# Attention steps of a fused two-block kernel: the values of a pair's first step are held back until those of its second

## What is computed

```python
# mixer A, one block of 128 queries over 512 keys (256 latents and 256 context)
s = jnp.einsum('bqhgd,bkhd->bhgqk', qi, k_all)
p = softmax_f32(s, v_all.dtype)
return jnp.einsum('bhgqk,bkhd->bqhgd', p, v_all)
# context queries, in the layers that need them
p = softmax_f32(jnp.einsum('bqhgd,bkhd->bhgqk', qcg, kc), vc.dtype)
yc = jnp.einsum('bhgqk,bkhd->bqhgd', p, vc)
# NSA: three branches of one head, each a masked softmax, gated and added
gate = jax.nn.sigmoid(g)
o = gate[..., 0:1] * o_cmp + gate[..., 1:2] * o_sel + gate[..., 2:3] * o_win
```

## Time and profile before

| what | value |
|---|---|
| median of three runs | 1896.64 us (1894.64 to 1898.02) |
| the profiled execution's own time | 1895.2 us |
| its span in the trace | 1893.4 us |
| PE busy | 1849.8 us, 98% of the span, 12748 matmuls |
| DVE busy | 1270.3 us, 67% |
| ACT busy | 1084.1 us, 57% |
| POOL busy | 95.9 us, 5% |
| turns L2422, 624 of them | 86.8 us busy, mean 280 ns |
| values L2452 of 128x128, 992 records | 69.6 us busy, mean 279 ns |
| spreads L2445, 88 of them | 21.7 us busy, mean 283 ns |
| ACT copies L1046 after turns | idle before them 83.3 us, 44 times, until L2422 |

### The profile page before, as it was taken

One profiled execution on the slowest core, in us unless ns is written; L12 is line 12 of the kernel. 1 busy time (PEld: TensorE's weight loads), 2 busy tenths in 40 slices (PEclk: granted clock), 3 DMA queues, 4 the chain that ended last, 5 costly groups with the idle time before them and its releaser, 6 DMA issues.

```text
span 1893.4 us, 33080 instructions
## 1 busy us (share of the span) xinstructions
PE 1849.8 (98%) x12748; PEld 1596.1 (84%) x12748; DVE 1270.3 (67%) x2139; ACT 1084.1 (57%) x1899; POOL 95.9 (5%) x83
## 2 busy tenths in 40 slices
PE   7999999999999999999999999999999999999998
PEld 5878878868788987888889988889888889998887
DVE  6663344477735569775677687767776677687765
ACT  5372264385726477774556567755774555567762
POOL 0000000004000005000000010000000000010001
PEclk9999999999999999999999999999999999999999
DMA  9232243232224213555532445545554542345443
GB/s 352 90 112 89 89 158 110 90 134 90 90 89 161 96 68 142 191 190 192 199 134 96 150 177 180 197 179 183 194 179 177 225 156 90 123 178 188 178 179 132
DMA packets 42565, 285.40 MB, mean 151 GB/s; under 512 B 4944, under 2 KB 6352, under 8 KB 9424
## 3 DMA queue, kind: packets, MB, share of 16 engines
q1 hardware_dynamic: 40832, 278.24, 40.4%
q0 software_dynamic: 1616, 5.52, 0.9%
HBM read 282.69 MB, written 1.05 MB: 150 GB/s over the span
## 4 chain that ended last, share of the span: by engine, by line
issue 49%; PE 41%; DVE 3%; POOL 3%; ACT 2%; DMA 1%; SPq 0%; DVEq 0%; POOLq 0%; ACTq 0%
PE bank L2211 7%; PE bank L2212 7%; PE bank L2213 7%; PE bank L2217 6%; PE bank L2218 3%; PE bank L2452 3%; PE bank L2422 2%; PE bank L2397 2%; POOL work L852 1%; PE bank L2313 1%; DVE panels_lo L1451 1%; DMA token_major<-weights 1%; POOL xT L895 1%; ACT work L1059 1%; ACT panels_hi L926 0%
## 5 line engine op out<-in xcount | busy, mean ns | idle before, releaser
L2217 PE MATMUL bank<-acts,panels_hi 128*128 128x512 f32 x2032 | 718.2, 399 | 3.5 <-DVE xT L1949 2.6
L1451 DVE TENSOR_TENSOR panels_lo<-raw_panels,panels_hi 128x1024 fp32r<-128x1024 f32 x468 | 577.8, 1252 | 186.6 <-ACT panels_hi L926 184.9
L926 ACT ACTIVATE panels_hi<-raw_panels 128x1024 fp32r<-128x1024 f32 x468 | 484.2, 1054 | 253.9 <-PE bank L2213 145.5
L2218 PE MATMUL bank<-acts,panels_lo 128*128 128x256 f32 x2032 | 569.4, 280 | 0.0
L2217 PEld LDWEIGHTS bank<-acts,panels_hi 128*128 128x128 f32 x2032 | 382.3, 188 | 98.1 <-DVE xT L1949 2.8
L2218 PEld LDWEIGHTS bank<-acts,panels_lo 128*128 128x128 f32 x2032 | 384.0, 189 | 0.2
L2211 PE MATMUL bank<-acts,panels_hi 128*128 128x256 f32 (+1 forms) x1112 | 349.5, 314 | 2.9 <-ACT gates L1403 1.2
L2212 PE MATMUL bank<-acts,panels_hi 128*128 128x256 f32 (+1 forms) x1112 | 344.3, 310 | 0.0
L2213 PE MATMUL bank<-acts,panels_lo 128*128 128x256 f32 (+1 forms) x1112 | 344.3, 310 | 0.0
L2211 PEld LDWEIGHTS bank<-acts,panels_hi 128*128 128x128 f32 x1112 | 211.8, 190 | 20.3 <-issue 3.9
L2213 PEld LDWEIGHTS bank<-acts,panels_lo 128*128 128x128 f32 x1112 | 211.9, 191 | 11.1
(11 more groups left out here) (282 smaller groups left out, 1961.0 us busy)
## 6 DMA issues: line engine op xcount, KB each, us to landing
raw_panels<-weights SPq DMA_DIRECT2D x252, 1024.0 KB, 4.8
token_major<-weights SPq DMA_DIRECT2D x4, 1024.0 KB, 8.7
near_bias<-rpb POOLq DMA_DIRECT2D x16, 256.0 KB, 3.4
xT<-xin SPq DMA_DIRECT2D x4, 512.0 KB, 5.9
gates<-weights SPq DMA_DIRECT2D x2, 1024.0 KB, 10.4
near_bias<-weights SPq DMA_DIRECT2D x4, 512.0 KB, 7.1
token_major<-weights SPq DMA_DIRECT2D x2, 512.0 KB, 12.8
out<-xT SPq DMA_DIRECT2D x4, 256.0 KB, 2.4
```

The costliest lines, as they stand in the source:

```text
L926: act.activation(slot_hi(n, a, b), raw_of(n, a, b), ACT.Copy).then_inc(hi_ready, 1)
L1451: dve.tensor_tensor(slot_lo(n, a, b), raw_of(n, a, b), slot_hi(n, a, b).bitcast(F32), ALU.subtract).then_inc(lo_ready, 1)
L2217: pe.matmul(bank.rearrange("p (c t) -> p c t", c=2), whi_, with_rest(xhi_), start=start, stop=False, skip_group_check=True)
L2218: return pe.matmul(bank[:, 0:T], wlo_, xhi_, start=False, stop=stop, skip_group_check=True)
```

## The change

In iteration i PE no longer issues spread and values of a pair's first step. It issues them one iteration later, with those of the second: first both spreads, then the values of the first step, then those of the second. Steps that are first and last at once stay where they were. No instruction is added or removed, and the code of ACT, DVE, POOL and SP is the same.

```diff
                 if blk == 2 and i == len(steps) + 2:
                     ahead(2)
-                if 0 <= j < len(steps):
+                if not 0 <= j < len(steps) or steps[j].first and not steps[j].last:
+                    ready = []
+                else:
+                    ready = [j] if steps[j].first else [j - 1, j]
+                for j in ready:
                     g, step = g0 + j, steps[j]
                     if late and j == 0:
                         pe.wait_ge(gate_last_out, late)
...
                         pe.wait_ge(normed, now(normed, 2 * g + 2))
                     for k, q0 in step.deferred:
                         pe.transpose(out_bank[:, T + q0:T + q0 + P], inverse_rows(blk, g, k), ident)
+                for j in ready:
+                    g, step = g0 + j, steps[j]
                     pe.wait_ge(probT_out, now(probT_out, g + 1))
                     if step.cmp:
                         pr = pairs[step.pair][0]
```

## The result

The changed kernel takes 1900.74 us (median of 20 runs, 1897.4 to 1905.83) against 1896.63 for the kernel before (20 runs, 1891.63 to 1902.44): a ratio of 1.0025, 95% interval 1.0017 to 1.0032, slower by 4.1 us. In a second group of runs it took 1902.2 against 1894.87, 1.0033 (1.0020 to 1.0046), 7.3 us. The forecast was +6.0. The profiled execution took 1900.34 us, its span is 1898.5 and its mean granted clock 0.996 (before: 1895.2, 1893.4, 0.998).

A forecast was written before the change was run, and what follows sets the result against it. PE, busy 98% of the span, was taken as the bound, with a 2.21 us floor from turns to turns through ACT's copy. 2.0 - 0.8 + 4.6 + 0.2 = +6.0 us gave 1902.6 us; 8-in-10 range 1898.5 to 1907.

The forecast's parts named there:

- (1): PE, every pair: fewer changes of tile shape, 0.09 us each; 2.9 us saved over 32 pairs at one change each.
- (2): PE's wait for the previous pair's output goes; 1.8 us idle in all until L1630, 0.38 of it at 419.14.
- (4): End of mixer C, layer 0: values hide in a wait for ACT and the output wait goes, -0.8 us.
- (3): Layer 0: ten bare iterations with scores behind cost +0.20 us a pair, +2.0 in all; copy's wait for values hidden.
- the bare iteration: Odd iteration left without spread and values: turns to turns takes 2.21 us, set by ACT's copy, for 1.92 of work.
- (5): Layer 1 mixers: first even turns stay put, values come after them; A +1.69, B +1.59, C +1.32, together +4.6 us.
- the pins: Layer 1 mixers: first even turns come no earlier if PE arrives earlier, as ACT rounds panels before its copy.
- (6): NSA: waits of 0 to 0.1 us against 0.09 saved, last pair about +0.4 a layer; +0.2 for both layers.
- Rival (c): NSA: ACT's later rounding delays the gates of all eight pairs, +4 to +6 us on top, 1908 us; chance 0.12.
- Rival (a): PE's scores and other work cover ACT's copy; only (1) and (2) are left, 1892 us; chance 0.06.
- Rival (b): Slack after mixers absorbs half the shift in layer 1 and A, B of layer 0: +2.9, 1899.5 us; chance 0.16.

The follow-up runs named there:

- e5: The change with values held back but not grouped (spread, values, spread, values): 1907.87 us, ratio 1.0064 to the kernel before.
- e2: The change with ACT's copy of the turned probabilities cut in two, one piece per head and bank: 1889.79 us, ratio 0.9975 to the kernel before.
- e4: The change with a third buffer for the copied probabilities in the first block: 1898.35 us, ratio 1.0025 to the kernel before.
- e1: The change, but with layer 1 of the first block left as before: 1895.46 us, ratio 1.0001 to the kernel before.
- e6: The change with a gate panel's rounding and split three iterations later in the first block: 1902.74 us, ratio 1.0042 to the kernel before.
- e9: The change with ACT's copy cut in two and a third probability buffer in the first block: 1887.61 us, ratio 0.9961 to the kernel before.
- e12: The change with cut copy and third buffer, values held back everywhere but in C of layer 1: 1889.31 us, ratio 0.9967 to the kernel before.
- e10: The kernel before with cut copy and third buffer, no values held back: 1891.03 us, ratio 0.9978 to the kernel before.
- e11: The change with cut copy and third buffer, values not held back in A of layer 0 and C of layer 1: 1889.76 us, ratio 0.9984.
- e8: The change run again without any edit: 1902.2 us, ratio 1.0033 to the kernel before.

## Why the prediction was right

The sign, the mechanism and the size held: +4.1 and +7.3 measured for +6.0, inside the range. By its steps:

- **(1) changes of shape, mis-sized.** I took 0.09 us for one change. Grouped, the stretch takes 2.20 and not the 2.26 I used, and ungrouped 2.51 (e5): two changes are worth 0.31. The Trainium skill, "TensorEngine Tiling (Array Packing)", Key Properties, says that a switch of mode drains TensorE and gives no size; here it is 0.15 between transposes and values. My 0.09 came from turns with scores behind them, another pair of shapes.
- **(2) waits for the output.** The one of 0.38 us at the end of C in layer 0 went. But the waits of spreads for L1630 fell only from 1.8 to 1.4, and I had written "nearly gone" as a sign: what is left stands in front of single steps (128.80, 132.41 and 292.16 in the changed trace). The sum used only the first, in (4).
- **(3) the bare iteration** is 2.21 to 2.22 us in 9 of the 10 places in layer 0 and at the second pair of all three mixers in layer 1, and cutting the copy brings 1.92 (e2). A pair in B of layer 0 costs 0.14 to 0.16 more (7.66 us for 7.50 to 7.52), forecast 0.20. In A of layer 0 three pairs cost as little, and the fourth, with its bare iteration of 3.16 us, 0.35. Its copy's wait for values is not hidden, because a rounding follows it on ACT, and costs 0.44 (e4); I had put this wait at nothing. So +0.73 for +0.8 in A is partly luck, B came at +0.57.
- **(4) end of C, layer 0**: the stage came at -0.54 for -0.4.
- **(5) layer 1**: the pins held to 0.01 us in A and C, counted from the start of the stage. From them, two pairs take 12.50 us in both (502.10 to 514.60 in A), forecast 12.60, and what stands behind came 0.24 shorter than I had it: four changes of shape at 0.15 and not 0.09. Together A +1.35 for +1.69, C +0.98 for +1.32. In B the pin did not hold: in e4 its first even turns come 4.37 us after the turns before, in the kernel before 4.63. That gives +0.96 (e4, no fall of the clock) for +1.59.
- **(6) NSA** came at -0.25 for +0.2. The wait at the last pair is there, as forecast: in the first of the two NSA stages it takes 0.30 us more than before (forecast about 0.4). But each of the other three pairs takes 0.14 to 0.16 less, where I had waits of 0 to 0.1 against a saving of 0.09. Rival (c), the NSA chain turned critical, did not appear.

Without the fall of the clock the stages sum to +3.8 (the change's row with e4's B of layer 1), 2.2 under the forecast. Most of it is (1): the mis-sized changes of shape make up 1.0 in layer 1 and about 0.06 a pair in layer 0, and very likely the NSA difference too, where nothing but shapes and waits changed. The uncovered wait in A of layer 0 went the other way. On top came a term that no step had, the clock in B of layer 1: that stage is 1.1 us longer than e4's in one profile and 3.1 in the other, of which 0.9 and 2.8 lie in the one stretch (from turns to turns 4.98 and 6.83 us, 4.04 in e4) in which the clock was low. The two errors have opposite signs, and part of the accuracy is their cancelling.

Rival (a), that the copy never bites, is what happens once the copy is cut; for this kernel spoke rightly against it. Rival (b) fell by e1 and by the distances between the stages.

## What to carry to other kernels

Work that looks movable on the bound engine may be what fills a chain through another engine: before moving it, compute the distance from each product to the next that reuses its banks without it. If that distance is set by one evacuation of several banks, cut the evacuation per bank first; here grouping products of one shape paid only then. Look also at what the other engine has in front of that evacuation: the places where this change cost more than its sum said had a rounding there. And read a small change off stages that repeat to 0.02 us, not off whole executions.

## What the runs showed of the hardware that I had not expected

**TensorE's clock can fall where its waits stand close together.** PE in mixer B of layer 1 of the changed kernel, and the time slices (stretch, its length, busy time and count of PE, PEld, DVE, ACT, POOL, then the granted clock, DMA share, GB/s):

```profile
604.06 1.09 PE L2422 MATMUL bank<-consts_sb,work 128*128 128x128 f32 x8 [0.23 <-ACT token_major L1046]
606.71 1.32 PE L2397 MATMUL bank<-kT_split,qT_split 64*128 64x512 f32 x6 [1.56 <-ACT work L1059]
608.57 1.97 PE L2422 MATMUL bank<-consts_sb,work 128*128 128x128 f32 x8 [0.54 <-ACT token_major L1046]
```

```profile
604.00:606.00 2.00, 1.09 (x8) 0.86 (x8) 1.58 (x5) 0.80 (x4) 0.00 (x0) 1.00 0.01 4
606.00:608.00 2.00, 1.29 (x6) 0.56 (x6) 1.79 (x9) 2.00 (x4) 0.54 (x1) 0.78 0.29 76
608.00:610.00 2.00, 1.46 (x9) 1.43 (x8) 2.00 (x5) 2.00 (x6) 0.54 (x1) 0.50 0.45 104
610.00:612.00 2.00, 2.00 (x27) 1.82 (x27) 1.90 (x5) 0.85 (x2) 0.54 (x1) 0.87 0.20 82
```

PE is busy 2.38 of the 4 us from 604, then the grant is 0.50, that is 1.2 instead of 2.4 GHz, and eight turns with what follows take 1.76 us (608.57 to 610.33) and not 0.94. The kernel before has a spread and values there:

```profile
604.53 0.33 PE L2445 MATMUL bank<-consts_sb,token_major 128*128 128x128 f32 x1 [1.12 <-DVE gates L1694]
604.79 1.09 PE L2452 MATMUL bank<-token_major 128*64 128x128 f32 x16
```

and its clock stays at 1.00 in this stage. In the change's second profile it fell again and for longer:

```profile
606.00:608.00 2.00, 0.97 (x6) 0.49 (x6) 1.89 (x8) 2.00 (x6) 0.54 (x1) 0.94 0.21 35
608.00:610.00 2.00, 1.29 (x6) 1.29 (x7) 1.86 (x3) 2.00 (x6) 0.54 (x1) 0.50 0.56 162
610.00:612.00 2.00, 2.00 (x16) 1.67 (x16) 1.90 (x7) 0.94 (x1) 0.54 (x1) 0.50 0.16 66
612.00:614.00 2.00, 2.00 (x22) 2.00 (x20) 0.39 (x1) 0.88 (x1) 0.00 (x0) 0.50 0.79 184
```

Of the five profiles with values held back in this stage and the copy in one piece, three have the fall there (the change twice, e6); none of the other nine has. That the missing values are the cause is the likely reading, not a shown one. It doesn't come each time: in e4 PE was busy 0.66 and 1.02 us in the two slices from 604 to 608 and the grant stayed at 1.00. A fall at the start of A of layer 1 (e5, e6, e9, e12) stands behind an idle time of PE of 1.8 us (493.61 to 495.40 in the kernel before) that the change has too. It came in four of the nine profiles that hold values back in that stage and in none of the five that don't; but it starts ahead of the first place where the holding back changes anything in the stage, so whether the two are connected is open.

**The same products run at one of two paces at full grant.** 100 us of the second block, the stretches from 760 and from 1140 us, in the kernel before:

```profile
760.00:860.00 100.00, 100.00 (x569) 86.68 (x568) 74.84 (x100) 67.80 (x98) 0.00 (x0) 1.00 0.53 189
1140.00:1240.00 100.00, 100.00 (x579) 87.42 (x578) 79.00 (x109) 73.42 (x109) 0.00 (x0) 1.00 0.52 189
```

and in the changed one:

```profile
760.00:860.00 100.00, 100.00 (x579) 88.15 (x578) 77.08 (x105) 70.95 (x104) 0.00 (x0) 1.00 0.55 197
1140.00:1240.00 100.00, 100.00 (x568) 86.69 (x567) 77.11 (x107) 72.38 (x107) 0.00 (x0) 1.00 0.52 188
```

569 or 579 matmuls, 1.8% apart, with a grant of 1.00 in all and no work of the change in either. All fourteen profiles show one of the two paces in each stretch (567 to 569 or 578 to 579), and the distances to the attention stages follow it:

| from | to | fast pace | slow pace |
|---|---|---|---|
| last values of C, layer 1 | first NSA scores | 278.9 to 279.2 us | 281.5 to 281.6 us |
| last values of the first NSA and MoBA stage | next NSA scores | 497.0 us | 500.2 us |
| last values of the second | end of the span | 242.3 to 242.4 us | 245.5 to 245.6 us |

A fall of the clock near 960 us (e10, e11) or near 1550 us (e5, e10, e12) adds 1.4 to 1.7 us to its row; the one that ten profiles show between 711 and 727 us, both kernels among them, adds nothing that can be seen. For the third I did not count matmuls; it takes one of two lengths, 3.2 us apart. The three together are 9 us between all fast and all slow, and that is where most of the 8 to 11 us between single executions of one kernel can come from. The kernel before and the change show it: their spans differ by 5.1 us, the stages by 4.9, and between them lie -2.6 and +3.2 from two stretches whose pace changed, and -0.4 ahead of the first stage. e9's profile (span 1884.4) is fast in all three, that of e10 (span 1897.0) slow in all three; e6's, fast in all three, is the fastest of its six executions, and e8's, slow in all three, the slowest of its five. What sets the pace was not tried.
